# Embedding outputs copied by ScalarE, an earlier bank wait for two products, and norm splits moved, in a two-layer hybrid encoder step on one core

## The chip, the cores and the metric

The kernel runs on one core of one Trainium2 chip. The metric is the device time of one execution in microseconds, as the median of several runs. TensorE multiplies, VectorE (DVE) and ScalarE (ACT) work element by element and read TensorE's results out of PSUM, GpSimd (POOL) works on SBUF only, and SyncE (SP) issues nearly all DMAs. Each engine runs its own instructions in the order of the program and waits on semaphores that the others raise.

## The reference

544 tokens (512 of a prompt and 32 of a sample) of width 1024 pass through two layers. A layer is

```
x = x + concat(A, B, C, D) @ w_out          # four mixers on rmsnorm(x) @ w_in
x = x + square(relu(rmsnorm(x) @ mlp_w1)) @ mlp_w2                   # 1024 -> 4096 -> 1024
x = x + (pl @ ple_w_proj) * sigmoid(rmsnorm(x) @ ple_w_gate)         # pl: 256 wide, one per layer
```

and a final rmsnorm gives y. All is float32. The change touches the end of the second line and the third one, the embedding block.

## The kernel before, in words

x lies in SBUF with features on partitions, as 8 tiles of 128x544 (tile m holds features 128m to 128m+127). A weight matrix is cut in units of 128 output features: a unit is 128x1024 float32, loaded by SP (`load_unit`, L675) into one of four raw places. Each float32 value is split in a high part (fp32r, made by ScalarE: `high`, L893, which waits for the product two units before to have left the place) and a remainder (made by POOL from raw and high: `rest`, L775). Activations are split likewise: `norm_high` (ACT, L958) scales a tile of x by the norm's gain, `norm_split` (DVE, L1237) makes the remainder; `square_x` (ACT, L964) and `add_square` (POOL, L801) gather the sum of squares, which TensorE sums over partitions (`sum_x`) and ScalarE turns into 1/rms (`inv_rms`, L970: a logarithm read from PSUM and an exponential); the product is multiplied by it afterwards. The two tiles of squares alternate, so square m waits until POOL has added square m-2.

A product (`product`, L1724) takes for each of 8 input tiles three matmul pairs (high by high, high by remainder, remainder by high; two halves of 272 tokens): 48 matmuls. Its output takes two of the four banks of psum_p, so outputs alternate between two slots, and output o waits for the evacuation of output o-2 (`evacuated`, L640, a count on the semaphore `freed`).

The MLP runs in 4 groups of 1024 hidden features. A group has 8 such products into psum_p and then 4 pairs (p = 0 to 3) of output tiles, each from seven half-size products (K_A11, K_S1, K_S2, K_S4, K_S3, K_A12, K_A22, in this order, 12 matmuls each: `pair_product`, L1762) into the four banks of the other PSUM tensor, psum_t, each waiting for the evacuation of the one four before. VectorE evacuates and adds them into x tiles 2p and 2p+1 (L1576 to L1598; A11 is copied by ScalarE, L915), and between them makes the weight sums for the next pair (`pair_sum`, L1520). A12 completes tile 2p, A22 tile 2p+1. In the last group VectorE also makes the norm splits for the embedding block, two in each of the pairs 1 to 3 (behind S2 and S4), and splits 6 and 7 at the end.

Then the embedding block, outputs from O_PLE on. Outputs 0 to 3 are products of the embedding with `ple_w_proj` (12 matmuls each, unit U_PLE), 4 to 7 gate products 0 to 3 (48 matmuls each, units U_PLE+1 to U_PLE+4), 8 to 11 again embedding products (U_PLE+5), 12 to 15 gate products 4 to 7. VectorE copies embedding outputs to `ple_out` (L1695, five tiles in turn), multiplies a gate output by 1/rms (L1702), ScalarE takes the sigmoid (L1208), VectorE multiplies by the embedding and adds to x (`add_gated`, L1680). ScalarE then squares the new x tile and, in layer 0, scales it for layer 1, and VectorE makes layer 1's split.

All orders are written out by hand in one function for each engine. POOL's order in the last group is: remainders due, then in pair p the sums of squares 2p-2 and 2p-1, with U_PLE's remainder ahead of sum 4, and U_PLE+1's behind sum 5. In layer 0 SP loads, behind U_PLE+2, the next layer's parameters (waiting for the last split) and 1088 KB of constants (L757), and then U_PLE+3.

## Time and profile before

| | us |
|---|---|
| runs (3), median | 1614.86 (1613.15 to 1617.97) |
| profiled execution, time | 1612.89 |
| profiled execution, span | 1611.1 |
| TensorE busy | 1525.2 (95%) |
| VectorE busy | 1050.8 (65%) |
| POOL busy | 832.0 (52%) |
| ScalarE busy | 670.0 (42%) |

The mean granted TensorE clock was 0.988 of full speed. The embedding block of layer 0 lies at about 736 to 805 us of the span, that of layer 1 at 1528 to 1594 us. In timelines a row gives start, duration, engine, line, what is written and read, how many instructions are merged, and in brackets the idle time before it with what ended it.

### The profile page before, as it was taken

The page shows a single profiled execution, that of the slowest core. Times are in us where ns is not written, and L with a number is a line of the kernel's source. Part 1 is how long each engine was busy: PE and PEld are TensorE (multiplying, and loading weights), DVE is VectorE, ACT ScalarE, POOL GpSimd, SP SyncE. Part 2 cuts the span into 40 slices and gives each one's busy share as a digit, 9 for nine tenths or more (in the row PEclk, how much of TensorE's full clock was granted, in tenths as well). Part 3 has the DMA queues.
Part 4 walks back from the last instruction along what each step waited for, and adds up shares of the span by engine and source line. Part 5 has one row for each costly group of instructions (what it writes and reads, how often), then busy time and mean ns, then how long its engine had stood idle before and what let it go on. Part 6 is the DMA issues. An engine that isn't in the chain of part 4 may idle for free.

```text
span 1611.1 us, 33871 instructions
## 1 busy us (share of the span) xinstructions
PE 1525.2 (95%) x14198; PEld 1439.6 (89%) x14198; DVE 1050.8 (65%) x1754; ACT 670.0 (42%) x1186; POOL 832.0 (52%) x467
## 2 busy tenths in 40 slices
PE   6999999899999999998999999998999999999896
PEld 6889787799999999988998897878999999999895
DVE  6865557656848567596677645664487584756954
ACT  6521433335544343453455223342454443434522
POOL 3344111165766849486543431112759486684943
PEclk9999999999999999999999999999999999999998
DMA  5211001152241414213322110113333224141221
GB/s 197 79 41 42 27 28 40 46 133 92 79 132 53 132 53 118 80 53 100 104 67 67 41 39 17 41 40 73 113 97 96 89 79 132 53 133 51 66 80 69
DMA packets 43960, 123.81 MB, mean 77 GB/s; under 512 B 10976, under 2 KB 13792, under 8 KB 43552
## 3 DMA queue, kind: packets, MB, share of 16 engines
q1 hardware_dynamic: 43664, 119.86, 24.1%
q8 instruction: 113, 1.85, 0.5%
q10 hardware_dynamic: 144, 1.78, 0.3%
q14 instruction: 39, 0.32, 0.1%
HBM read 117.86 MB, written 3.76 MB: 75 GB/s over the span
## 4 chain that ended last, share of the span: by engine, by line
PE 73%; DVE 18%; issue 3%; ACT 3%; POOL 1%; DMA 0%; SPq 0%; POOLq 0%; DVEq 0%; ACTq 0%
PE psum_p L1736 37%; PE psum_t L1777 16%; PE psum_p L1791 5%; PE psum_t L1827 5%; DVE conv_out L1277 2%; DVE hidden L1241 2%; PE psum_p L1970 1%; PE psum_p L1950 1%; PE psum_p L1756 1%; PE psum_t L1943 1%; PE psum_t L1938 1%; POOL w_rest L779 1%; DVE probs L1491 1%; DVE x L1588 1%; DVE mla_q L1308 1%
## 5 line engine op out<-in xcount | busy, mean ns | idle before, releaser
L1736 PE MATMUL psum_p<-hidden,w_high 128*128 128x272 f32 x3776 | 637.6, 291 | 10.9 <-POOL w_rest L779 8.6
L1736 PEld LDWEIGHTS psum_p<-hidden,w_high 128*128 128x128 f32 x3776 | 537.0, 189 | 15.6 <-POOL w_rest L779 10.3
L779 POOL TENSOR_TENSOR w_rest<-raw,w_high 128x1024 fp32r<-128x1024 f32 x114 | 280.5, 2464 | 464.9 <-ACT w_high L899 464.9
L1736 PE MATMUL psum_p<-hidden,w_rest 128*128 128x272 f32 x1888 | 391.2, 289 | 0.0
L1736 PEld LDWEIGHTS psum_p<-hidden,w_rest 128*128 128x128 f32 x1888 | 296.9, 189 | 0.0
L791 POOL TENSOR_TENSOR w_rest<-w_sums,w_high 128x512 fp32r<-128x512 f32 x128 | 207.7, 1648 | 93.3 <-DVE w_sums L1533 55.3
L899 ACT ACTIVATE w_high<-raw 128x1024 fp32r<-128x1024 f32 x114 | 120.1, 1055 | 192.4 <-PE psum_p L1736 115.4
L1777 PE MATMUL psum_t<-hidden_split_a,w_high 128*128 128x272 f32 x896 | 178.5, 290 | 12.8 <-issue 7.7
L1777 PE MATMUL psum_t<-hidden_split_b,w_high 128*128 128x272 f32 x896 | 177.1, 288 | 0.4 <-DVE hidden_split_b L1549 0.4
L1777 PEld LDWEIGHTS psum_t<-hidden_split_a,w_high 128*128 128x128 f32 x896 | 140.0, 188 | 17.3 <-issue 17.1
L1777 PEld LDWEIGHTS psum_t<-hidden_split_b,w_high 128*128 128x128 f32 x896 | 140.3, 188 | 0.8 <-DVE hidden_split_b L1549 0.8
L1777 PE MATMUL psum_t<-hidden_split_b,w_rest 128*128 128x272 f32 x448 | 128.9, 288 | 0.0
L1777 PE MATMUL psum_t<-hidden_split_a,w_rest 128*128 128x272 f32 x448 | 128.8, 288 | 0.0
L913 ACT ACTIVATE w_high<-w_sums 128x512 fp32r<-128x512 f32 x128 | 79.6, 628 | 118.0 <-DVE w_sums L1531 62.4
L1557 DVE SCALAR_TENSOR_TENSOR rope_in<-psum_p,rms 128x544 f32<-128x544 f32 x64 | 46.2, 722 | 114.8 <-PE psum_p L1736 102.7
L779 POOL TENSOR_TENSOR w_rest<-raw_more,w_high 128x1024 fp32r<-128x1024 f32 x32 | 80.4, 2521 | 54.1 <-ACT w_high L899 54.1
L1241 DVE SCALAR_TENSOR_TENSOR hidden<-x,parameters,hidden 128x544 fp32r<-128x544 f32 x48 | 78.6, 1642 | 32.7 <-ACT hidden L962 32.0
L938 ACT ACTIVATE hidden_parts<-rope_in 128x544 f32<-128x544 f32 x64 | 42.2, 659 | 127.7 <-DVE rope_in L1557 127.7
L1791 PE MATMUL psum_p<-hidden,w_high 128*128 128x272 f32 x512 | 91.2, 300 | 0.1
L791 POOL TENSOR_TENSOR w_rest<-raw,w_high 128x512 fp32r<-128x512 f32 x48 | 75.0, 1570 | 29.0 <-ACT w_high L913 29.0
L1777 PEld LDWEIGHTS psum_t<-hidden_split_b,w_rest 128*128 128x128 f32 x448 | 84.3, 188 | 0.0
L1777 PEld LDWEIGHTS psum_t<-hidden_split_a,w_rest 128*128 128x128 f32 x448 | 84.3, 188 | 0.0
(289 smaller groups left out, 2578.0 us busy)
## 6 DMA issues: line engine op xcount, KB each, us to landing
raw<-w_units SPq DMA_DIRECT2D x146, 512.0 KB, 3.6
raw_more<-w_units SPq DMA_DIRECT2D x64, 512.0 KB, 3.6
x<-x_t SPq DMA_DIRECT2D x8, 272.0 KB, 6.3
y_t<-y SPq DMA_DIRECT2D x8, 272.0 KB, 2.1
constants<-consts ACTq DMA_DIRECT2D x1, 1737.5 KB, 8.1
ple_in<-p_t SPq DMA_DIRECT2D x2, 544.0 KB, 11.0
constants<-consts SPq DMA_DIRECT2D x1, 1088.0 KB, 5.3
w_kv<-w_kv SPq DMA_DIRECT2D x2, 256.0 KB, 5.2
```

The source lines that it names most:

```text
L779: mark(pool.tensor_tensor(wlo_at(l, s, 2), raw_at(l, u), whi_at(l, s, 2).bitcast(F32), ALU.subtract), lo_done)
L791: mark(pool.tensor_tensor(wlo_at(l, s, 1), src, whi_at(l, s, 1).bitcast(F32), ALU.subtract), lo_done)
L899: mark(act.activation(whi_at(l, place_of(u), 2), raw_at(l, u), ACT.Copy), hi_done)
L913: mark(act.activation(whi_at(l, s, 1), src, ACT.Copy), hi_done)
L938: link(act, act.activation(dst, two(xr[:]), ACT.Square), h_sq, l)
L1241: mark(dve.scalar_tensor_tensor(ha[l][:, m, 1, :], x[:, m, :], g, f(ha[l][:, m, 0, :]), ALU.mult, ALU.subtract), normed)
L1277: step(dve.scalar_tensor_tensor(dst, src[:, j:j + cols], w, dst, ALU.mult, ALU.add), l)
L1557: link(dve, dve.scalar_tensor_tensor(two(xr[:]), psum_of(l, o), 0.0, two(rms[:]), ALU.max, ALU.mult), freed, l)
L1736: ins = pe.matmul(pp[:, 2 * b + h, 0:HALF], w(l, s, 2)[:, cols(k)], rhs[:, k, part, h * HALF:(h + 1) * HALF], start=(n == 0 and z == 0), s ...
L1777: ins = pe.matmul(bank, w(l, s, 1)[:, j * P:(j + 1) * P], hs(l, j)[:, half, part, :], start=(j == 0 and z == 0), stop=(j == PAIRS - 1 and ...
L1791: ins = pe.matmul(pp[:, h, 0:HALF], w(l, s, 2)[:, k * P:(k + 1) * P], ha[l][:, k, half, h * HALF:(h + 1) * HALF], start=(k == 0 and z == 0 ...
L1827: ins = pe.matmul(dst[r, j * C:(j + 1) * C], lhsT(r), rhs(r), start=True, stop=True)
```

## The change

- `copy_ple` is new: ScalarE copies embedding output m from PSUM to `ple_out` and signals `ple_copied`. Copies 0 to 3 stand around the scaling and squaring of x tiles 6 and 7, copies 4 to 7 in the loop over gates behind the sigmoid of gate 3 (4 and 5) and behind the square and scaling of tile 3 (6 and 7). VectorE's copies go; `add_gated` of tile 3 moves to its own turn.
- `evacuated` counts the embedding outputs on `ple_copied`, and the first two embedding products wait for the last hidden product of the last group, the last reader of psum_p, instead of the outputs two before them.
- The splits of tiles 0 to 5 in the last group stand at (pair 1, S4), (2, S2), (2, S4), (3, S2), (3, S4), (3, S3) instead of two in each pair; POOL adds square 5 behind U_PLE+1's remainder instead of ahead of it.

```diff
@@ -473,7 +473,7 @@
         lo_done = signal("lo_done", O_PLE + 2 + KT, 4)
         sums = signal("sums", 4 * PAIRS * GROUPS)
         proj = signal("proj", OUTPUTS, 2)
-        freed = signal("freed", OUTPUTS - PAIRS * GROUPS, 2)
+        freed = signal("freed", OUTPUTS - PAIRS * GROUPS - KT, 2)
         x_high = signal("x_high", 3 * KT)
         normed = signal("normed", 3 * KT, 1)
 
@@ -554,7 +554,7 @@
         ple_hi = signal("ple_hi", 1)
         copied = signal("copied", PAIRS * GROUPS)
         ple_sp = signal("ple_sp", 1)
-        ple_o = signal("ple_o", 2 * KT)
+        ple_copied = signal("ple_copied", KT)
         gate_in = signal("gate_in", KT)
         gated = signal("gated", KT)
         yd = signal("yd", 0)
@@ -644,6 +644,9 @@
             for g in range(GROUPS):
                 for p in range(PAIRS):
                     before += pair_out(g, p, K_A11) <= o
+            if O_PLE <= o < O_PLE + 4 or O_PLE + 8 <= o < O_PLE + 12:
+                return ple_copied.at(l, o - O_PLE + 1 - (4 if o >= O_PLE + 8 else 0))
+            before += (4 if o >= O_PLE + 4 else 0) + (4 if o >= O_PLE + 12 else 0)
             return freed.at(l, o + 1 - before)
 
         def square_no(phase, m):
@@ -864,8 +867,10 @@
                         rest_of(l, due(g, 2 * KT + 7 * p, ahead))
                         if g == GROUPS - 1 and p:
                             add_square(l, 2, 2 * p - 2)
-                            add_square(l, 2, 2 * p - 1)
+                            if p < PAIRS - 1:
+                                add_square(l, 2, 2 * p - 1)
                         rest_of(l, due(g, 2 * KT + 7 * p + ahead, 7 - ahead))
+                add_square(l, 2, KT - 3)
                 add_square(l, 2, KT - 2)
                 add_square(l, 2, KT - 1)
                 u = U_PLE + SPLIT
@@ -919,6 +924,12 @@
                     q = PAIRS * g + p - 1
                     act.wait_ge(*evacuated(l, pair_out(q // PAIRS, q % PAIRS, K_S4)))
                 mark(act.activation(pq[:, 0, :], pair_bank(g, p, K_A11), ACT.Copy), copied)
+
+            def copy_ple(l, m):
+
+                o = O_PLE + m + (4 if m >= 4 else 0)
+                act.wait_ge(*proj.at(l, o + 1))
+                mark(act.activation(two(pout[:, m % 5, :]), out_of(l, o), ACT.Copy), ple_copied)
 
             def high_of(l, work):
 
@@ -1189,9 +1200,14 @@
                                 for m in (2 * p - 2, 2 * p - 1):
                                     norm_high(l, 2, m)
                                     square_x(l, 2, m)
-                for m in (KT - 2, KT - 1):
-                    norm_high(l, 2, m)
-                    square_x(l, 2, m)
+                copy_ple(l, 0)
+                copy_ple(l, 1)
+                norm_high(l, 2, KT - 2)
+                square_x(l, 2, KT - 2)
+                copy_ple(l, 2)
+                norm_high(l, 2, KT - 1)
+                square_x(l, 2, KT - 1)
+                copy_ple(l, 3)
                 for m in range(KT):
                     if m % 4 == 0:
                         high(l, U_PLE + SPLIT + 5 * (m // 4))
@@ -1206,12 +1222,18 @@
                         high(l + 1, u - UNITS)
                     act.wait_ge(*gate_in.at(l, m + 1))
                     mark(act.activation([xr, sqt][m % 2][:], [xr, sqt][m % 2][:], ACT.Sigmoid), gated)
+                    if m == 3:
+                        copy_ple(l, 4)
+                        copy_ple(l, 5)
                     if m < KT - 1:
                         square_x(l, 3, m)
                         if l + 1 < DEPTH:
                             if m == 0:
                                 act.wait_ge(*gains_in.at(l + 1, 16))
                             norm_high(l + 1, 0, m)
+                    if m == 3:
+                        copy_ple(l, 6)
+                        copy_ple(l, 7)
 
             act.preload_act_table_set(nat)
             square_x(DEPTH, 0, KT - 1)
@@ -1549,6 +1571,8 @@
                 mark(dve.tensor_tensor(hs(l, j)[:, 1, a:b, :], hq[:, a:b, :], f(hs(l, j)[:, 0, a:b, :]), ALU.subtract),
                      hidden)
 
+            norms = {(1, K_S4): 0, (2, K_S2): 1, (2, K_S4): 2, (3, K_S2): 3, (3, K_S4): 4, (3, K_S3): 5}
+
             def mlp_group(l, g):
                 for i in range(KT):
                     o = mlp_out(g, i)
@@ -1594,8 +1618,8 @@
                             dst = {K_S4: x[:, m, HALF:TOK], K_A12: x[:, m, 0:HALF], K_A22: x[:, m + 1, 0:HALF]}[k]
                             link(dve, dve.tensor_tensor(dst, bank, dst, ALU.add), freed, l)
                         sums_of(l, due(g, 2 * KT + 7 * p + k, 1))
-                        if g == GROUPS - 1 and p and k in (K_S2, K_S4):
-                            norm_split(l, 2, m - 2 + (k == K_S4))
+                        if g == GROUPS - 1 and (p, k) in norms:
+                            norm_split(l, 2, norms[p, k])
                 if g == GROUPS - 1:
                     norm_split(l, 2, KT - 2)
                     norm_split(l, 2, KT - 1)
@@ -1684,25 +1708,18 @@
                             dve.wait_ge(*gains_in.at(l + 1, 16))
                         norm_split(l + 1, 0, m - 1)
                     dve.wait_ge(*gated.at(l, m + 1))
+                    dve.wait_ge(*ple_copied.at(l, m + 1))
                     step(dve.tensor_tensor(gate, gate, pout[:, m % 5, :], ALU.mult), l)
                     link(dve, dve.tensor_tensor(x[:, m, :], x[:, m, :], gate, ALU.add), x_new, l)
 
                 for m in range(KT):
-                    if m % 4 == 0:
-                        for j in range(4):
-                            o = O_PLE + 2 * m + j
-                            dve.wait_ge(*proj.at(l, o + 1))
-                            link(dve, dve.tensor_copy(two(pout[:, (m + j) % 5, :]), psum_of(l, o)), freed, l)
-                        if m:
-                            add_gated(m - 1)
-                        if m == 0:
-                            dve.wait_ge(*rms_ready.at(l, 3))
+                    if m == 0:
+                        dve.wait_ge(*rms_ready.at(l, 3))
                     o = O_PLE + 4 * (m // 4 + 1) + m
                     dve.wait_ge(*proj.at(l, o + 1))
                     link(dve, dve.tensor_tensor(two([xr, sqt][m % 2][:]), psum_of(l, o), two(rms[:]), ALU.mult), freed, l)
                     mark(dve.memset(t1[:, 0:1], 0.0), gate_in)
-                    if m % 4 < 3 or m == KT - 1:
-                        add_gated(m)
+                    add_gated(m)
 
             dve.wait_ge(rms_ready.sem, DEPTH * rms_ready.per + 1)
             for m in range(KT):
@@ -1725,7 +1742,7 @@
 
                 b, s = slot(l, o), place_of(u)
                 pe.wait_ge(*lo_done.at(l, weight_no(u) + 1))
-                pe.wait_ge(*evacuated(l, o - 2))
+                pe.wait_ge(*evacuated(l, mlp_out(GROUPS - 1, KT - 1) if o in (O_PLE, O_PLE + 1) else o - 2))
                 for n, k in enumerate(order):
                     if between is not None and n == len(order) // 2:
                         between()
```

## Rows read from the trace of the kernel before

**Rows 1.** The page, its parts 1 and 4, whole span: busy time by engine; last chain.
```profile
PE 1525.2 (95%) x14198; PEld 1439.6 (89%) x14198; DVE 1050.8 (65%) x1754; ACT 670.0 (42%) x1186; POOL 832.0 (52%) x467
...
PE 73%; DVE 18%; issue 3%; ACT 3%; POOL 1%; DMA 0%; SPq 0%; POOLq 0%; DVEq 0%; ACTq 0%
```

**Rows 2.** Timeline of TensorE, layer 1: start us, us, what, count, idle before and releaser.
```profile
1513.97 0.49 PE L1777 MATMUL psum_t<-hidden_split_a,w_high 128*128 128x272 f32 x2 [1.52 <-DVE x L1595]
...
1525.02 0.29 PE L1777 MATMUL psum_t<-hidden_split_b,w_rest 128*128 128x272 f32 x1
1528.30 0.74 PE L1736 MATMUL psum_p<-ple_split,w_high 128*128 128x272 f32 x4 [2.99 <-DVE x L1595]
...
1531.44 1.11 PE L1736 MATMUL psum_p<-ple_split,w_high 128*128 128x272 f32 x4
...
1534.38 0.74 PE L1736 MATMUL psum_p<-ple_split,w_high 128*128 128x272 f32 x4 [1.37 <-DVE ple_out L1695]
...
1537.44 0.67 PE L1736 MATMUL psum_p<-hidden,w_high 128*128 128x272 f32 x4
...
1543.21 0.41 PE L1736 MATMUL psum_p<-hidden,w_rest 128*128 128x272 f32 x2
...
1575.48 0.77 PE L1736 MATMUL psum_p<-hidden,w_high 128*128 128x272 f32 x4 [0.85 <-POOL w_rest L779]
```

**Rows 3.** Windows, layer 1: stretch, us, busy (count) by engine, clock, DMA share, GB/s.
```profile
1530.00:1532.00 2.00, 2.00 (x11) 2.00 (x10) 2.00 (x2) 0.67 (x2) 2.00 (x2) 0.50 0.00 0
```

**Rows 4.** Timeline of VectorE, layer 1.
```profile
1500.09 1.34 DVE L1241 SCALAR_TENSOR_TENSOR hidden<-x,parameters,hidden 128x544 fp32r<-128x544 f32 x1
...
1521.26 1.77 DVE L1241 SCALAR_TENSOR_TENSOR hidden<-x,parameters,hidden 128x544 fp32r<-128x544 f32 x1
...
1523.42 2.48 DVE L1241 SCALAR_TENSOR_TENSOR hidden<-x,parameters,hidden 128x544 fp32r<-128x544 f32 x1
...
1527.71 0.92 DVE L1595 TENSOR_TENSOR x<-psum_t,x 128x272 f32<-128x272 f32 x2
1529.04 4.55 DVE L1241 SCALAR_TENSOR_TENSOR hidden<-x,parameters,hidden 128x544 fp32r<-128x544 f32 x2 [0.41 <-ACT hidden L962]
```

**Rows 5.** Timeline of POOL, layer 1.
```profile
1522.42 2.90 POOL L779 TENSOR_TENSOR w_rest<-raw,w_high 128x1024 fp32r<-128x1024 f32 x1
...
1531.18 3.61 POOL L811 TENSOR_TENSOR x_squares_summed<-x_squares_summed,x_squared 128x544 f32<-128x544 f32 x2
1538.84 2.39 POOL L779 TENSOR_TENSOR w_rest<-raw,w_high 128x1024 fp32r<-128x1024 f32 x1 [4.05 <-ACT w_high L899]
```

**Rows 6.** Timeline of ScalarE, layer 1.
```profile
1523.11 1.05 ACT L899 ACTIVATE w_high<-raw 128x1024 fp32r<-128x1024 f32 x1
...
1537.70 1.06 ACT L899 ACTIVATE w_high<-raw 128x1024 fp32r<-128x1024 f32 x1 [7.03 <-PE psum_p L1736]
1544.58 0.71 ACT L973 ACTIVATE rms<-psum_t,constants 128x544 f32<-128x544 f32 x1 [5.82 <-PE psum_t L1721]
...
1563.68 0.64 ACT L1208 ACTIVATE squares<-squares 128x544 f32<-128x544 f32 x1
```

**Rows 7.** Instructions on ple_out, both layers: duration ns min/median/max, first and last start.
```profile
L1695 DVE COPY ple_out<-psum_p x16: 711/725/726, 741.6 to 1568.7; 128x544 f32<-128x544 f32 x16
...
L1687 DVE TENSOR_TENSOR squares<-squares,ple_out x8: 721/2474/2753, 761.7 to 1595.5; 128x544 f32<-128x544 f32 x8
```

**Rows 8.** Timeline of VectorE, layer 0.
```profile
771.28 0.72 DVE L1702 TENSOR_TENSOR squares<-psum_p,rms 128x544 f32<-128x544 f32 x1
```

**Rows 9.** Part 6 of the page, and SP's queue, layer 0: the constants' transfer.
```profile
constants<-consts SPq DMA_DIRECT2D x1, 1088.0 KB, 5.3
...
742.04 0.43 SPq L757 DMA_DIRECT2D constants<-consts  x1
```

**Rows 10.** Timeline of TensorE, layer 0.
```profile
784.70 0.77 PE L1736 MATMUL psum_p<-hidden,w_high 128*128 128x272 f32 x4 [1.81 <-POOL w_rest L779]
...
785.60 1.11 PE L1736 MATMUL psum_p<-hidden,w_high 128*128 128x272 f32 x4
```

## The prediction

> **What bounds the kernel now.** I read the page's busy shares first: TensorE is busy 95% of the span, and the chain that ended last is 73% TensorE and 18% VectorE [rows 1]. So time is to be had only where TensorE stands still, and I looked for that around the edited code: the last MLP group and the embedding block, which run once in each of the two layers, at 690 to 805 us and at 1480 to 1594 us. The layers agree in what follows to about 0.1 us after a shift of 792 us; I work in layer 1's times.
>
> TensorE's timeline there [rows 2] shows four larger stops. A pair product is 12 matmuls in about 1.5 us (the last ends at 1525.31). At 1513.97 it has waited 1.52 us for a VectorE evacuation. The first embedding product starts only at 1528.30, 2.99 us after it, released by an evacuation into x, though it writes a bank of the other PSUM tensor. After the stop the second product runs at half clock: in 1530 to 1532 the granted clock is 0.50, the lower level, 1.2 GHz [rows 3]. Then TensorE stands 1.37 us until VectorE has copied the first product out; products 3 and 4 take 1534.38 to 1537.4, and gate product 0 takes 1537.44 to 1543.45, so 6.02 us for 48 matmuls. From 1525.31 to 1537.44 are 12.13 us, in which TensorE has 48 matmuls, 6.02 us of work. The fourth stop, 0.85 us at 1575.48 (about 1.1 by the starts of the matmuls), waits for POOL's weight remainder.
>
> Why VectorE is late is in its rows [rows 4]: in this stretch hardly one has idle time before it, evacuations, weight sums and norm splits in a row. At the end, 1529.04 to 1533.6, it runs splits 6 and 7 (4.55 us for both) before it takes the first embedding copy.
>
> **The change, part by part.**
>
> *New wait for the first two products.* They wait for the bank's last reader, the evacuation of the last hidden product, some 50 us back. What is late next is the weight remainder of U_PLE: POOL writes it at 1522.42 to 1525.32, and POOL's rows here, as those before them, have no idle time in front, down to 1534.79 [rows 5]. So TensorE can start at about 1525.4 instead of 1528.30: 2.9 us gained. Nothing else is queued behind that wait but the following products.
>
> *Splits spread.* Splits 0 to 5 sat at two each in pairs 1, 2, 3; now one, two, three, the last behind the S3 addition. Pair 1 loses one split, 1.34 us by its row [rows 4]. VectorE has a backlog there, so every evacuation up to pair 2's last comes up to 1.34 us earlier and the pair products end at about 1524.0. That buys nothing as long as POOL delivers U_PLE at 1525.3; it is cover for POOL's being quicker where VectorE is idle (gain 0 to 0.3 us, I take 0). The added split falls between the S3 addition and the A12 evacuation: 1.34 to 2.48 us by the neighbours; I take 1.77, the split at 1521.26 with POOL beside it [rows 4]. Net of the 1.34 us before it, x tiles 6 and 7 come at 1528.6 and 1529.1 instead of 1528.15 and 1528.63.
>
> *Copies on ScalarE.* The trace has no ScalarE copy of 128x544 from PSUM with this form; nearest is the logarithm out of PSUM, 0.71 us [rows 6]; VectorE's copies take 0.711 to 0.726 [rows 7]. I take 0.71 (bounds 0.64, the sigmoid of the same shape [rows 6], and 0.75). ScalarE is in order: U_PLE+1's high part is done at 1524.15. Product 1 runs 1525.4 to 1526.9, copy 0 to 1527.8; product 2 to 1528.4, copy 1 to 1529.35; product 3 starts at 1528.4 and product 4 at 1529.9, both without a stop. Scaled tile 6 (0.7) and its square (0.6) then run to 1530.65, copy 2 to 1531.35. Gate product 0 needs that bank: 1531.5, where TensorE is free at 1531.45. Splits 6 and 7 end at about 1532.3 and 1534.5 and are needed 4.5 and 5.3 us into gate 0, at 1536.0 and 1536.8: covered. POOL: square sum 4 to 1527.1, U_PLE+1's remainder to 1529.7 (now ahead of sum 5), sums 5, 6, 7 to 1534.9, U_PLE+2's remainder (2.39) to 1537.3; wanted at 1538.2 after the sum of squares. Covered by 0.9 us. So gate 0 starts 5.95 us earlier than 1537.44.
>
> *Second four embedding products.* Gate 3 ends near 1562.5 (1543.45, the sum of squares 0.7, three gates and a slower restart of 0.2). Copies 4 and 5 follow the sigmoid of tile 3 (ends 1564.32) and keep up. Copies 6 and 7 sit behind the square of x tile 3, which waits for VectorE's gate multiply, 2.5 us beside POOL [rows 7], and its addition: 1567.6, square 1568.3, copy 6 at 1569.0. Gate 4 then starts 0.65 us late. In exchange VectorE no longer holds x tile 3 back behind its four copies, to about 1571, so U_PLE+7 is converted in time and the stop at 1575.48 (1.1 us) goes. Net gain 0.45. Layer 1 in all: 5.95 + 0.45 = 6.4 us; its tail after the last gate is unchanged.
>
> *Layer 0 differs* in this block, since VectorE also makes the next layer's splits and multiplies take up to 2.75 us beside POOL [rows 7]: it reaches gate 3's output at 771.28, late by 0.8 us against 770.5, gate 3's end [rows 8]. And the constants' transfer, issued at 742.04 behind the last split, stands in front of U_PLE+3's load [rows 9]; the last split now ends about 1.0 us later (742.6), so, with 5.3 us for the constants and an estimated 0.5 for the rest of the load behind them, the load lands near 748.9, while ScalarE, after the rms (1544.58 and 1.4 us, less the two shifts), wants it at 748.05. That shifts the multiply chain by 0.85 us. With it I get stops of 0.3 (U_PLE+5's remainder), 0.7, 1.25 (copy 4 after a late sigmoid) and 1.2 us (copy 6 behind square and scaled tile 3), together 3.45, where today are 0.35 at product 2 and at gate 5 a stop of 1.81 us followed by 3.6 us at low clock, some 1.7 lost [rows 10]: 3.9. Gain 0.45 minus 0.1 for gate 2, plus 5.95 before it: 6.2 us.
>
> Sum: 6.4 + 6.2 = 12.6; I take off 0.3 for semaphore latencies that I rounded away: 12.3. The profiled execution took 1612.89 us (span 1611.1), so 1600.6; the runs' median, 1614.86, lies 2 us above it, and 12.3 below the median is 1602.5.
>
> On the splits beside POOL: the rows show 1.34 and 2.48 us for one shape. The Trainium skill (SBUF — State Buffer, "Who interferes with whom") says that a VectorE instruction with two SBUF inputs and a GpSimd instruction that reads SBUF lock each other out for a whole instruction. By it the added split could wait for one whole weight remainder and take 2.5 us instead of 1.77; copy 2 and gate 0 would be 0.7 us later in each layer, 1.4 in all, and the time 1603.9.
>
> **Rivals.**
>
> *A, the clock falls all the same.* TensorE would still stand about 1.4 us before the first product. For: 1.81 us before 784.70 was enough, the clock fell 0.6 us after it [rows 10]. Against: 1.52 us at 1513.97 was not [rows 2]. Price: at low clock six matmuls take 1.36 us instead of 0.75 (a group of four 1.11 against 0.67) [rows 2]; the stretches lasted 3.6 us, 1.6 to 1.8 us lost each. Once per layer, and once for layer 0's stops at the second four: 5.0 us, time 1607.5.
>
> *B, a queue is behind.* POOL has no gap, and U_PLE+2's remainder has 0.9 us of slack only. If it came as now, 1541.23, gate 1 would start 1541.3 instead of 1538.2: 3.1 us lost per layer, gain 12.3 - 6.2 = 6.1, time 1608.8. Against: that time is set today by the 7.03 us ScalarE waits for the product [rows 6], which goes.
>
> *C, no change.* The copies do not keep up: if ScalarE reached copies 0 and 1 only behind tiles 6 and 7, product 3 would again wait until about 1532.5, and the second four would lose the rest. The program order puts them first, so this is that the change doesn't do what it says. Time 1614.
>
> *D, slower.* The stops of layer 0 at the second four are close together (0.7, 1.25, 1.2 us between products of 1.5 us). If they hold the clock at 1.2 GHz not for 3.6 us but through gates 4 to 7, each gate takes 10.9 us instead of 6.02: 19.5 us more, time 1622. It decides from 12.3 / 0.81 = 15 us of TensorE work, two and a half gates, done at the low level. Against: both falls in this stretch ended after 3.6 us, once work went on.
>
> **How the numbers follow.** Forecast 64% (own range 1599 to 1605.5), A 19%, B 9%, C 4%, D 4%. Range for 8 in 10: below to 1598.5 (POOL quicker by 0.3 per layer, copies at 0.64, the median's own scatter of 2 us), above to 1608, which takes in A. 0.3% of the time is about 4.8 us, what a measurement here can tell from no change: faster is the forecast, A, and B: 0.92; same 0.04; slower 0.04.
>
> **What would show it.** After: the first embedding product within 0.3 us of U_PLE's remainder, no 2.99 us stop and no clock of 0.50 there; four copies on ScalarE at 0.7 us; gate 0 about 6 us after the first product; the 1.52 us stop at pair 3 near 0.2; a stop of about 0.7 us ahead of gate 4 in layer 1 and of three about 1 us in layer 0; no stop ahead of gate 5. Wrong would be: first product not before 1528 (another release), copies over 1 us, gate 1 waiting for POOL, or a low clock for long.

## The result and the profile after

The changed kernel took 1604.33 us (median of 6 runs, 1600.98 to 1606.62) where the kernel before took 1613.8 (6 runs, 1611.09 to 1617.97): a ratio of 0.9936, interval 0.9922 to 0.995. Once more, on another occasion (e11 below), it was 1603.55 us and 0.9938 [0.9926, 0.9951]. So it is faster by some 10 us, where 12.3 were forecast. The profiled execution took 1600.98 us (span 1599.2), 11.9 less than the profiled one of before, and is the quickest of its six. Of the five executions of e5 below one took 3071.51 us: the median given there counts it, the ratio leaves it out, and the median of the other four is 1600.08 us.

First the page of the changed kernel, its parts 1 and 4, as [rows 1] of before: TensorE has 8.2 us less busy time with the same 14198 matmuls; most of it is time at the lower clock that is gone (6.8 us of clock less, by the sums under e11); VectorE has 16 instructions less, ScalarE 16 more.

```profile
PE 1517.0 (95%) x14198; PEld 1433.4 (90%) x14198; DVE 1041.9 (65%) x1738; ACT 678.2 (42%) x1202; POOL 832.2 (52%) x467
...
PE 72%; DVE 18%; ACT 5%; issue 3%; DMA 1%; POOL 1%; SPq 0%; POOLq 0%; DVEq 0%; ACTq 0%
```

TensorE's timeline in layer 1, to be laid beside [rows 2]. Its columns are start us, duration us, engine, line, what, count, and in brackets the idle time before and its releaser.

```profile
1506.53 0.49 PE L1794 MATMUL psum_t<-hidden_split_a,w_high 128*128 128x272 f32 x2 [1.60 <-DVE x L1619]
...
1517.59 0.29 PE L1794 MATMUL psum_t<-hidden_split_b,w_rest 128*128 128x272 f32 x1
1519.65 0.75 PE L1753 MATMUL psum_p<-ple_split,w_high 128*128 128x272 f32 x4 [1.78 <-issue]
1520.23 0.41 PE L1753 MATMUL psum_p<-ple_split,w_rest 128*128 128x272 f32 x2
...
1525.71 0.67 PE L1753 MATMUL psum_p<-hidden,w_high 128*128 128x272 f32 x4
...
1557.56 0.74 PE L1753 MATMUL psum_p<-hidden,w_high 128*128 128x272 f32 x4 [0.68 <-ACT ple_out L932]
```

The reader should see four things. The stop in front of the first embedding product is 1.78 us and no longer 2.99. The first four embedding products, 48 matmuls, run in 6.06 us without a stop (1519.65 to 1525.71). The stop before pair 3 (1506.53) has stayed. The granted clock, which was 0.50 in this place before [rows 3], is 1.00 (a window: stretch, its length, busy time and count by engine, clock, DMA share, GB/s):

```profile
1520.00:1522.00 2.00, 2.00 (x19) 2.00 (x18) 1.97 (x3) 0.57 (x1) 2.00 (x2) 1.00 0.54 162
```

What releases the first product reads "issue", which names nothing. GpSimd's timeline gives it: the remainder of weight unit U_PLE ends at 1519.55, 0.1 us before the product.

```profile
1513.09 3.66 POOL L814 TENSOR_TENSOR x_squares_summed<-x_squares_summed,x_squared 128x544 f32<-128x544 f32 x2
1516.71 2.84 POOL L782 TENSOR_TENSOR w_rest<-raw,w_high 128x1024 fp32r<-128x1024 f32 x1
1519.50 1.85 POOL L814 TENSOR_TENSOR x_squares_summed<-x_squares_summed,x_squared 128x544 f32<-128x544 f32 x1
1521.31 2.90 POOL L782 TENSOR_TENSOR w_rest<-raw,w_high 128x1024 fp32r<-128x1024 f32 x1
```

ScalarE's timeline shows the copies, each behind its product, and in the second four the square of tile 3 in front of the last two; the row under them is from the view by tile, with durations in ns (min/median/max) of all sixteen:

```profile
1521.43 0.63 ACT L932 ACTIVATE ple_out<-psum_p 128x544 f32<-128x544 f32 x1 [2.98 <-PE psum_p L1753]
1522.92 0.63 ACT L932 ACTIVATE ple_out<-psum_p 128x544 f32<-128x544 f32 x1 [0.87 <-PE psum_p L1753]
...
1556.24 0.66 ACT L979 ACTIVATE x_squared<-x 128x544 f32<-128x544 f32 x1 [1.69 <-DVE x L1713]
1556.81 1.12 ACT L932 ACTIVATE ple_out<-psum_p 128x544 f32<-128x544 f32 x2
...
L932 ACT ACTIVATE ple_out<-psum_p x16: 602/616/627, 736.7 to 1557.3; 128x544 f32<-128x544 f32 x16
```

Layer 0's second four products have stops of the kind that was forecast, at TensorE; there is none ahead of gate 5, where [rows 10] had 1.81 us:

```profile
768.44 0.74 PE L1753 MATMUL psum_p<-ple_split,w_high 128*128 128x272 f32 x4 [0.43 <-DVE squares L1720]
...
771.01 0.74 PE L1753 MATMUL psum_p<-ple_split,w_high 128*128 128x272 f32 x4 [0.85 <-ACT ple_out L932]
...
775.80 0.74 PE L1753 MATMUL psum_p<-hidden,w_high 128*128 128x272 f32 x4 [1.56 <-ACT ple_out L932]
```

Absolute times drift between executions, so I count from the first pair product of the last MLP group (1477.56 in layer 1 before, 1471.77 after). From there the places of one kernel agree within 0.1 us in both layers and in each profile, but for e1's gate 0. For every kernel of this study (us after that product; worked out from TensorE's timelines; layer 0 / layer 1 where they differ):

| kernel | pairs end | first product | gate 0 |
|---|---|---|---|
| before | 47.75 | 50.7 | 59.85 |
| changed | 46.1 | 47.85 | 53.9 |
| e1, wait alone | 47.8 | 47.85 | 62.35 / 61.3 |
| e2, copies alone | 47.75 | 50.7 | 59.5 |
| e3, change with the old splits | 47.75 | 47.85 | 53.9 |
| e4, splits alone | 46.1 | 50.6 | 58.55 |
| e6, e8, e12 | 46.1 | 46.1 | 52.5 |
| e9, old splits on e8 | 47.75 | 47.6 | 53.75 |
| e10, split 1 later on e8 | 46.0 | 46.1 | 52.5 |

(e5, e7 and e11 stand as the changed kernel.) VectorE's multiply of the last gate came 119.0 and 116.4 us after the start before, 113.2 and 110.2 after: 5.84 us gained in layer 0 and 6.13 in layer 1, together 12.0. That the two profiles differ by as much, 11.9, is luck: outside these stages there are differences of about 2 us both ways (under e11).

### The profile page after: what moved, and what is told of

Same layout as the page of the kernel before. It is cut to its first block, busy times and chain, and to the rows that moved or that the text cites. A ratio compares the mean times of both kernels' runs of the same rounds, so it can differ in the third digit from the quotient of the medians.

```text
span 1599.2 us, 33873 instructions
## 1 busy us (share of the span) xinstructions
PE 1517.0 (95%) x14198; PEld 1433.4 (90%) x14198; DVE 1041.9 (65%) x1738; ACT 678.2 (42%) x1202; POOL 832.2 (52%) x467
## 3 DMA queue, kind: packets, MB, share of 16 engines
q10 hardware_dynamic: 144, 1.78, 0.3%
## 4 chain that ended last, share of the span: by engine, by line
PE 72%; DVE 18%; ACT 5%; issue 3%; DMA 1%; POOL 1%; SPq 0%; POOLq 0%; DVEq 0%; ACTq 0%
PE psum_p L1753 35%; PE psum_t L1794 17%; PE psum_p L1808 5%; PE psum_t L1844 5%; DVE conv_out L1299 2%; PE psum_p L1773 1%; PE psum_p L1987 1%; PE psum_p L1967 1%; PE psum_t L1960 1%; PE psum_t L1955 1%; ACT w_high L904 1%; DVE probs L1513 1%; DVE squares L1712 1%; DVE w_sums L1559 1%; DVE mla_q L1330 1%
## 5 line engine op out<-in xcount | busy, mean ns | idle before, releaser
L1263 DVE SCALAR_TENSOR_TENSOR hidden<-x,parameters,hidden 128x544 fp32r<-128x544 f32 x48 | 75.0, 1565 | 32.8 <-ACT hidden L973 32.2
L794 POOL TENSOR_TENSOR w_rest<-raw,w_high 128x512 fp32r<-128x512 f32 x48 | 75.1, 1570 | 29.0 <-ACT w_high L918 29.0
```

Of the source, the lines that this page charges most:

```text
L794: mark(pool.tensor_tensor(wlo_at(l, s, 1), src, whi_at(l, s, 1).bitcast(F32), ALU.subtract), lo_done)
L1263: mark(dve.scalar_tensor_tensor(ha[l][:, m, 1, :], x[:, m, :], g, f(ha[l][:, m, 0, :]), ALU.mult, ALU.subtract), normed)
```

## The experiments

The first four take the change apart, each on the same chip beside the kernel before (1613.18 us, median of 25 runs). The next four alter one thing in the changed kernel or all three together (before: 1613.05, 9 runs), the last four follow up (before: 1613.66, 11 runs).

**e1: the new wait alone**, in the kernel before.

```diff
-                pe.wait_ge(*evacuated(l, o - 2))
+                pe.wait_ge(*evacuated(l, mlp_out(GROUPS - 1, KT - 1) if o in (O_PLE, O_PLE + 1) else o - 2))
```

> The kernel before with one edit: the first two embedding products wait for the last hidden product's evacuation. Copies stay on VectorE, splits stay two in each pair. My theory (the parts need each other): the first two products move up to U_PLE's remainder at about 1525.4, but product 3 waits as before for VectorE's first copy, which stands behind splits 6 and 7 that end at 1533.6; TensorE stands about 6 us in one piece there instead of 2.99 + 1.37, the clock falls to 0.50 behind it and gate 0 starts where it did or up to 1.8 us later. Time 0 to 4 us above before, ratio 1.000 to 1.002. Rival (each part gives its own share): the 2.9 us at the first product are gained in each layer, time 5.8 us below before, ratio 0.996.

Measured: 1617.92 us, ratio 1.0029 [1.0015, 1.0042]: slower. TensorE's timeline in layer 1 and a window of it:

```profile
1526.93 0.74 PE L1736 MATMUL psum_p<-ple_split,w_high 128*128 128x272 f32 x4
...
1535.88 1.25 PE L1736 MATMUL psum_p<-ple_split,w_high 128*128 128x272 f32 x4 [5.72 <-DVE ple_out L1695]
```
```profile
1537.00:1539.00 2.00, 2.00 (x11) 2.00 (x11) 0.00 (x0) 0.00 (x0) 0.00 (x0) 0.50 0.00 0
```

The first two products start at once when the pairs end. But VectorE's copies still stand behind the evacuations and splits 6 and 7, so TensorE stands 5.72 us in one piece in front of the third, and the work behind it runs at the clock of 0.50, 1.2 GHz. The windows show that clock for 6.8 us, from 1532.3 to 1539.1, where the kernel before has it for 3.4 us in this place; gate 0 comes 1.4 to 2.5 us later than before, which is more than I had expected. The wait alone moves a stop and makes it cost more.

**e2: the copies on ScalarE alone.** The cut shows two places of the edit to the kernel before.

```diff
+                copy_ple(l, 0)
+                copy_ple(l, 1)
...
-                            link(dve, dve.tensor_copy(two(pout[:, (m + j) % 5, :]), psum_of(l, o)), freed, l)
```

> The changed kernel with the other two parts undone: ScalarE's copies only; the first products wait for the outputs two before, splits two in each pair. My theory: the first product still starts near 1528.3 (layer 1, times of the kernel before), 3 us stop and low clock as before (some 1.3 us), then products 3 and 4 follow without the stop of 1.37 and the wait behind the splits: gate 0 near 1535.7 instead of 1537.44, 1.7 us gained; at the second four 0.45 in layer 1 and up to 2 in layer 0. Together 5 to 6 us below before, ratio 0.9965. Rival (the copies carry the whole gain and the early wait is only shifted waiting): as the changed kernel, ratio 0.9936.

Measured: 1611.47 us, 0.9991 [0.9978, 1.0004]. I had expected 0.9965, a miss. TensorE and a window:

```profile
1525.69 1.25 PE L1751 MATMUL psum_p<-ple_split,w_high 128*128 128x272 f32 x4 [2.94 <-DVE x L1617]
1526.73 0.66 PE L1751 MATMUL psum_p<-ple_split,w_rest 128*128 128x272 f32 x2
1527.18 1.11 PE L1751 MATMUL psum_p<-ple_split,w_high 128*128 128x272 f32 x4
```
```profile
1529.00:1531.00 2.00, 2.00 (x10) 2.00 (x10) 0.00 (x0) 0.41 (x1) 0.00 (x0) 0.50 0.63 166
```

The stop of 2.94 us is there, the stop for the copy (1.37 us in [rows 2]) is gone. But the clock is at 0.50 from the first product on and each four matmuls take 1.11 us for 0.66, so the four products need 8.8 us and not 6.05. The windows give a granted clock of 0.50 for 6.8 us (1524.9 to 1531.7), 6.0 of them with work, at a cost of 2.75 us. In the kernel before it is 0.50 for 3.4 us only (1529.5 to 1532.9), a cost of 1.7; it begins 1.2 us behind the start of the first product, and it is over when the second stop comes:

```profile
1533.00:1535.00 2.00, 0.63 (x6) 0.66 (x6) 1.95 (x3) 0.00 (x0) 1.64 (x2) 1.00 0.48 176
```

So 1.0 of the 1.37 us that the copies win goes into a longer stretch at the lower clock, and gate 0 gains 0.35 us. Layer 0 shows the same 6.8 and 3.4 us. The stop in front is as long in both kernels (2.94 and 2.99 us); why the stretch is twice as long in e2 is not shown.

**e3: the changed kernel with the splits at their old places.** GpSimd's sum 5 goes back ahead of the unit's remainder too, which the cut leaves out.

```diff
-            norms = {(1, K_S4): 0, (2, K_S2): 1, (2, K_S4): 2, (3, K_S2): 3, (3, K_S4): 4, (3, K_S3): 5}
+            norms = {(1, K_S2): 0, (1, K_S4): 1, (2, K_S2): 2, (2, K_S4): 3, (3, K_S2): 4, (3, K_S4): 5}
```

> The changed kernel with the splits back at two in each of pairs 1 to 3 and square 5 added ahead of U_PLE+1's remainder. My theory: POOL's remainder of U_PLE, not the end of the pair products, lets the first embedding product start, so the spread of the splits is worth nothing: pair products end 1.2 us later, the first product starts at the same time relative to the group's start, within 0.3 us of the changed kernel per layer; the stop before it shrinks from 1.78 to about 0.4 us. Ratio to before 0.9925 to 0.9945. If long stops now and then drop the clock in the changed kernel (its six runs lie in two groups, 1601 to 1603 and 1606 to 1607), this one has fewer of the slow ones. Rival (the spread matters): 1.2 us per layer lost, ratio 0.995 or above.

Measured: 1601.88 us, 0.9929 [0.991, 0.9948], not to be told from the change. The pairs end 1.65 us later, the first product starts at the same 47.85 us:

```profile
1519.24 0.29 PE L1792 MATMUL psum_t<-hidden_split_b,w_rest 128*128 128x272 f32 x1
1519.62 0.74 PE L1751 MATMUL psum_p<-ple_split,w_high 128*128 128x272 f32 x4
```

None of its four runs (1600.94 to 1602.13) is near 1606, as I had expected if the stop mattered; e6 below speaks against it. So the wait and the copies are the gain, and only as a pair: the ratios of e1 and e2 multiply to 1.0020.

**e4: the splits alone.** The same line of norms (and GpSimd's sum 5 behind the unit's remainder) in the kernel before.

> The kernel before with the splits' new places and POOL's new order alone. My theory: the pair products end 1.2 us earlier, but the first embedding product still waits for the A12 evacuation, which comes 0.0 to 0.5 us later than before because a split stands in front of it: time 0 to 1.5 us above before, ratio 1.000 to 1.001. Rival (the spread matters by itself): 1.2 us per layer gained, ratio 0.9985.

Measured: 1611.45 us, 0.9986 [0.9972, 1.0], which leaves the rival standing. Splits 6 and 7 on VectorE took 3.37 us for two, not 4.55 [rows 4], so the first copy came sooner; gate 0 gains 1.3 us in each layer. I had given this part nothing.

```profile
1530.98 3.37 DVE L1243 SCALAR_TENSOR_TENSOR hidden<-x,parameters,hidden 128x544 fp32r<-128x544 f32 x2 [0.41 <-ACT hidden L964]
```

**e5: the second four copies in one row**, in the changed kernel. The two lines go away in their old place, which the cut leaves out.

```diff
                     if m == 3:
                         copy_ple(l, 4)
                         copy_ple(l, 5)
+                        copy_ple(l, 6)
+                        copy_ple(l, 7)
```

> The changed kernel with one edit: ScalarE copies the second four embedding products one behind the other, 6 and 7 directly behind 4 and 5, ahead of the square and the scale of tile 3. My theory says that the stop in front of gate 4 (0.68 us in layer 1, 0.85 and 1.56 us in layer 0 of the changed kernel) is the two operations of 0.6 to 1.1 us between copies 5 and 6, so the stops go and each layer gains 0.7 to 1.5 us: 2 us of 1604, a ratio to the kernel before of 0.9925 where the change alone had 0.9936. Rival 1: what is late next is the square of tile 3 and through it the gate, VectorE then stops for ScalarE, and nothing is gained (0.9936). Rival 2: the stops are short enough to cost their own length only and the rest is other jitter, 0.9930.

Measured: 1601.39 us, 0.9924 [0.9908, 0.9939]. ScalarE's copies now stand one behind the other, and gate 4 has no stop in either layer, 0.85 us sooner in layer 1 and 1.74 in layer 0, as expected. The other stop for a copy in layer 0, 0.84 us before the third of the four products, stays. The comparison with 0.9936 alone would not tell it; the timeline does.

```profile
1551.94 0.63 ACT L932 ACTIVATE ple_out<-psum_p 128x544 f32<-128x544 f32 x1 [0.82 <-PE psum_p L1752]
1553.43 0.62 ACT L932 ACTIVATE ple_out<-psum_p 128x544 f32<-128x544 f32 x1 [0.87 <-PE psum_p L1752]
1554.92 0.63 ACT L932 ACTIVATE ple_out<-psum_p 128x544 f32<-128x544 f32 x1 [0.87 <-PE psum_p L1752]
```

**e6: the unit's remainder ahead of sum 3** on GpSimd, and ScalarE's square 5 behind its second copy. The cut shows GpSimd's part.

```diff
+                            if p == PAIRS - 1:
+                                add_square(l, 2, 2 * p - 3)
...
-                            if p < PAIRS - 1:
+                            if p < PAIRS - 2:
```

> The changed kernel with one edit in two places: GpSimd takes the embedding unit's remainder (2.90 us) ahead of the sum of square 3 (1.85 us), and ScalarE's square 5 goes behind its second copy. My theory says that the first embedding product's stop of 1.78 us at the end of the pairs is the place of that remainder in GpSimd's queue: it ends 1.85 us sooner, the stop goes in both layers, and gate 0 comes sooner by what the sums of squares allow. Time: 1.8 us by two layers less if the whole of it arrives, a ratio of 0.991 to 0.992; and the lower clock, which I take for the cause of the slower half of the changed kernel's runs (1606 against 1601 us, mean clock 0.989 against 0.992), should not be seen, so that all of its runs are near 1598. Rival 1: VectorE's splits decide the start of gate 0 (they end at the same time as before), the stop moves behind the eighth product, and the ratio stays at 0.9936. Rival 2: the slower half has nothing to do with this stop, and is seen here too.

Measured: 1601.31 us, 0.9922 [0.9907, 0.9937]. The stop of 1.78 us is gone: on TensorE the first product now follows the last pair product, and has no idle time in its row.

```profile
1514.05 0.29 PE L1798 MATMUL psum_t<-hidden_split_b,w_rest 128*128 128x272 f32 x1
1514.34 0.75 PE L1757 MATMUL psum_p<-ple_split,w_high 128*128 128x272 f32 x4
```

Of the 1.75 us, gate 0 keeps 1.4 (52.5 against 53.9), and 0.6 more is lost by the end of gate 3, where TensorE now stops 0.22 us for the next remainder and restarts slower. The slower half of its runs is there still (1600.6 to 1602.6 at a mean clock near 0.989, the quick one 1596.4 at 0.993). So rival 2 of this expectation holds: my idea that this stop lets the clock fall in half of the runs is wrong. At the last gate 0.6 us is left in layer 0 and 1.1 in layer 1, not 1.8 in each.

**e7: the next layer's loads one unit later.**

```diff
-                    if u == U_PLE + 2 and l + 1 < DEPTH:
+                    if u == U_PLE + 3 and l + 1 < DEPTH:
```

> The changed kernel with one edit: SyncE issues the next layer's parameters and constants one unit later, behind the transfer of the raw weights that ScalarE waited for in layer 0 (0.69 us). My theory prices this at 0 to 0.7 us, since it comes once in the kernel and ScalarE's work there is not what TensorE waits for last: ratio 0.9934, not to be told from the change (0.9936). The rival, that this transfer's lateness is what puts the stops of 0.4 to 1.6 us into layer 0 behind its second four products, expects them gone and 2.5 us less: 0.992.

Measured: 1601.45 us, 0.9929 [0.9916, 0.9942]. In the timelines of ScalarE, layer 0, the wait for the raw weights is in the changed kernel's row and not in e7's:

```profile
750.18 1.06 ACT L904 ACTIVATE w_high<-raw 128x1024 fp32r<-128x1024 f32 x1 [0.69 <-DMA raw<-w_units]
```
```profile
749.40 1.05 ACT L904 ACTIVATE w_high<-raw 128x1024 fp32r<-128x1024 f32 x1
```

Of the stops in layer 0's second four, the two in front of the first and the second product (0.24 and 0.43 us) go, those for a copy stay at 0.83 and 1.56 us. Gate 4 comes 0.8 us sooner, about what my theory priced.

**e8: e5, e6 and e7 together.**

> The changed kernel with the three edits together: four copies in one row, the embedding unit's remainder ahead of sum 3, the next layer's loads one unit later. If the stops are separate places, their gains add: 2 us of the copies, 3.6 us of the remainder, up to 0.7 us of the loads, so 1598 us and a ratio of 0.990. If the sums of squares or VectorE take the place of each stop that goes, it stays at 0.993.

Measured: 1594.77 us (1592.47 to 1598.76), 0.989 [0.9872, 0.9908]. The gains add: counted at the last gate, e5, e6 and e7 gain 1.8, 0.6 and 0.8 us over the change in layer 0 and 0.9, 1.1 and 0.0 in layer 1, 5.2 in sum, and e8 gains 3.9 and 1.8, so 5.7. **e12, the same kernel again** beside the change:

> The kernel with three further edits once more, on the same chip as the change: 0.989 to the kernel before and 9 to 10 us below the change if the first comparison was right, which had 4 runs alone; between 0.990 and 0.991 if its two quick runs were luck.

Measured: 1595.52 us, 0.9895 [0.9877, 0.9913]; it lies 8.0 us below the changed kernel on the same chip, where the last gates give 5.7; the rest is not explained by these stages. It beats both kernels.

**e9: e8 with the splits at their old places** (the edit of e3).

> The kernel with the three further edits, with the norm splits of the last group at their old places (pairs' products 1_S2, 1_S4, 2_S2, 2_S4, 3_S2, 3_S4) again. In the changed kernel the new places were worth nothing, since GpSimd's remainder set the first embedding product whenever the pairs ended. My theory says that with the remainder out of the way the pairs' end sets it, so the old places now cost what they delay it by, 1.2 us in each layer: 2.4 us more than the kernel with three edits, a ratio of 0.9905 against its 0.989. The rival, that VectorE has the same work before gate 0 whatever its order, expects gate 0 at the same distance from the group's start and the same time, 0.989.

Measured: 1597.91 us, 0.9908 [0.9894, 0.9923], 2.4 us slower than e12 on the same chip, where the two intervals overlap. The timelines decide: pairs end at 47.75, gate 0 at 53.75 against 52.5, and the last gate comes 1.2 us later in layer 0 and 0.7 in layer 1. So the new places of the splits are worth 1.2 us at gate 0, and 1.9 us in the two layers together, from the moment the stop behind them goes, and nothing before.

**e10: e8 with split 1 behind S4 and split 2 behind S3.**

```diff
-            norms = {(1, K_S4): 0, (2, K_S2): 1, (2, K_S4): 2, (3, K_S2): 3, (3, K_S4): 4, (3, K_S3): 5}
+            norms = {(1, K_S4): 0, (2, K_S4): 1, (2, K_S3): 2, (3, K_S2): 3, (3, K_S4): 4, (3, K_S3): 5}
```

> The kernel with the three further edits, with VectorE's split 1 moved from behind pair 2's product S2 to behind its S4, and split 2 to behind S3. TensorE stops 1.58 us in front of pair 3 for an addition that stands behind split 1 (1.69 us) in VectorE's order. If the order is what counts, the stop goes and each layer gains up to 1.6 us: a ratio of 0.987 against 0.989. If VectorE's work paces the pairs, smaller stops in pair 3 take it over and the pairs end no more than 0.3 us sooner: 0.989. The second is what the changed kernel did with its splits, and I give it two chances in three.

Measured: 1598.76 us (1592.86 to 1602.24), 0.9908 [0.9893, 0.9924], not to be told from e12 by the intervals; the last gates stand where e12's do, within 0.1 us. The stop in front of pair 3 went, and one of 1.69 us came in front of that pair's third product; the pairs end 0.1 us sooner:

```profile
1507.91 0.49 PE L1797 MATMUL psum_t<-hidden_split_a,w_high 128*128 128x272 f32 x2
...
1512.99 0.49 PE L1797 MATMUL psum_t<-hidden_split_a,w_high 128*128 128x272 f32 x2 [1.69 <-DVE x L1622]
```

The first row is the start of pair 3, 33.14 us after the group's first pair product (34.73 in e8), with no idle time. So the order of these two splits decides where TensorE stands still, and VectorE's work as a whole when the pairs end: the second case of the expectation, but for the one stop of the old length where I had expected smaller ones.

**e11: the changed kernel again.**

> The changed kernel once more, beside the kernel with three further edits on the same chip. Expected: 0.9936 again, runs from 1600 to 1607 us. The clock's falls outside the embedding stage lie at other places in every profile so far (25, 245, 260, 310, 340, 815, 1100 us), each worth some 1.7 us; if they are what spreads the runs of one kernel over 5 us, this profile shows other places than the first one did, and its time stands to the first profile's as their number does. If something in the embedding stage spreads the runs, both profiles differ there.

Measured: 1603.55 us, 0.9938 [0.9926, 0.9951]. In both its profiles the clock is 1.00 all through the embedding stage. The expectation's second half is a miss. This profile has the first one's falls (at 310, 815 and 1100 us) and one more at 260; by the sums below it loses 3.4 us more to the clock, and yet it took 0.4 us less (1600.57 against 1600.98 us). One place where the lost time is made up lies in layer 0. At 323 us this execution is 2.2 us behind the first one (325.46 against 323.29 us for the same product). Then both wait for a weight remainder in front of one product, the first execution for 3.30 us and this one for 0.77, since ScalarE gets the raw weights of that unit at nearly the same time in both (335.38 and 334.98 us):

```profile
338.91 0.77 PE L1753 MATMUL psum_p<-hidden,w_high 128*128 128x272 f32 x4 [3.30 <-POOL w_rest L782]
```
```profile
338.55 0.77 PE L1753 MATMUL psum_p<-hidden,w_high 128*128 128x272 f32 x4 [0.77 <-POOL w_rest L782]
```

So time lost to the clock can vanish in a later wait for weights, and the clock is not all that counts. Most of what spreads the runs is outside the embedding stage, best seen in the two profiles of e8 and e12, one kernel, 9.2 us apart (1593.03 and 1602.23). Windows of e8:

```profile
28.00:30.00 2.00, 2.00 (x10) 2.00 (x10) 1.96 (x4) 1.98 (x3) 2.00 (x1) 0.50 0.53 217
340.00:345.00 5.00, 5.00 (x42) 5.00 (x42) 2.75 (x2) 1.33 (x3) 3.38 (x3) 1.00 0.36 116
1100.00:1105.00 5.00, 4.69 (x38) 4.47 (x36) 2.15 (x2) 2.46 (x4) 2.09 (x1) 1.00 0.00 0
```

and of e12:

```profile
28.00:30.00 2.00, 2.00 (x18) 2.00 (x18) 1.96 (x4) 1.98 (x3) 2.00 (x1) 1.00 0.58 234
340.00:345.00 5.00, 5.00 (x28) 5.00 (x29) 3.70 (x3) 2.30 (x3) 5.00 (x3) 0.66 0.33 107
1100.00:1105.00 5.00, 5.00 (x30) 4.53 (x30) 0.45 (x2) 0.29 (x2) 0.00 (x0) 0.50 0.45 77
```

Summed over windows of 5 us up to the last gates, (1 - clock) times 5 us gives 5.1 us lost in e8's profile and 15.4 in e12's, a difference of 10.3 where the times differ by 9.2. (It counts idle time in a window too, so it is an upper estimate.) The same sum, in the embedding stages of both layers (715 to 800, 1500 to 1570 us) and elsewhere: before 5.1 and 6.8; e1 6.9 and 6.8; e2 6.8 and 6.7; e4 5.2 and 10.2; the change 0 and 5.1, again (e11) 0 and 8.5; e3 0 and 6.8; e5 to e10 0 and 3.4 to 13.6. In all 14 profiles the clock falls between 305 and 320 us and between 1090 and 1110 us; the other places differ from one execution to the next. Each is worth 1.7 us or more by this sum, and only those of the embedding stage belong to the change.

## Why the prediction was right, and where it was not

**New wait, first product at the remainder's end: right.** 2.9 us were forecast; the first product moved from 50.7 to 47.85 us after the group's start. GpSimd's remainder ends at 47.8 us in both kernels.

**Splits spread, earlier pairs worth nothing: right for the change.** e3 shows the same first product and gate 0 without it. The pairs end 1.65 us sooner, not 1.2 to 1.34. The step "the 1.52 us stop at pair 3 near 0.2" is wrong: it is 1.60 us, and e10, which takes it away in front of pair 3, gets it back inside that pair; what vanished in the change are the smaller stops in front of and within pair 2, some 1.7 us in all. With the old kernel's copies the part is worth more than I saw (e4), and with the remainder out of the way too (e9).

**Copies on ScalarE, gate 0 5.95 us earlier: right.** 5.95 by the table. The copies take 0.60 to 0.63 us, not 0.71. e1 and e2 show that this gain is neither part's own: one gives GpSimd's time as the start, the other takes the copies off VectorE, and alone each leaves a long stop with a low clock behind it.

**Second four, layer 1: a stop of 0.65 before gate 4 and none before gate 5: right**, 0.68 and none. **Layer 0: right in kind.** Forecast 0.3, 0.7, 1.25 and 1.2 us; from the starts of the matmuls 0.24, 0.6, 1.0 and 1.74. e7 shows which of them hang on the late load (0.69 us at ScalarE, 0.85 forecast): the first two. e5 shows that the last is the square and the scaled tile in front of copy 6.

**The sum, 12.3 us: near in the edited stages, 2 to 3 us too much for the medians.** The stages give 5.84 and 6.13, so 12.0. (The prediction's own terms for layer 0, 0.45 - 0.1 + 5.95, make 6.3 and not 6.2.) The term that came out small is the second four: in layer 1 the stops and the stop that goes leave 0.19 us where 0.45 was forecast, in layer 0 they leave 0.14 for 0.45, and 0.27 is lost ahead of them where 0.1 was. The gain is at the first four alone.

The medians differ by 9.5 and 10.1. What they lack lies outside the edited stages, which the prediction took as equal in both kernels. The clock there is the likeliest cause and not a proven one: it costs 3.4 to 15.4 us in one execution and another, and among the six executions of the change the time goes with the mean clock (0.993 took 1600.98 us; 0.991 took 1601.29 and 1602.74; 0.990 took 1605.92; 0.989 took 1606.18 and 1606.62). A single profile of before says little of it. Whether the change also makes these falls likelier is open; 14 profiles do not tell. The two profiled executions agree with the stages' 12.0 by luck: the changed kernel's loses 1.7 us less to the clock outside them, and waits 2.1 us longer for the weights at 338 us (3.30 against 1.18). Luck helps the forecast time as well: 1602.5 was counted from a median of three runs, 1614.86, that lies 1.1 to 1.8 us above the later ones.

**Rivals.** A, the clock falls all the same: no, in neither profile of the changed kernel nor in those of e3 and e5 to e10. B, a queue behind: GpSimd's U_PLE+2 remainder began at 1529.09 and gate 1 had no stop. C and D did not come about. A's price may have been too low: the stretch at the lower clock, which the prediction took as 3.6 us, is 3.4 by the windows in the kernel before, but 6.8 in e1 and e2. The stop of 1.78 us is as long as the one of 1.81 us in [rows 10] behind which the clock fell, and in e1 a stop of 1.81 us at the place of [rows 10] left the clock at 1.00; what tells them apart is not shown here.

**The split beside GpSimd.** Before, a split that starts at 1523.42 ends at 1525.90, 0.58 us after the remainder beside it, which ends at 1525.32 [rows 4, 5]. In the changed kernel VectorE's rows read:

```profile
1515.91 1.42 DVE L1263 SCALAR_TENSOR_TENSOR hidden<-x,parameters,hidden 128x544 fp32r<-128x544 f32 x1
1517.25 0.43 DVE L1614 TENSOR_TENSOR pair_parts<-psum_t,pair_parts 128x272 f32<-128x272 f32 x1
1517.72 2.42 DVE L1615 TENSOR_TENSOR x<-x,pair_parts 128x544 f32<-128x544 f32 x1
1520.17 1.77 DVE L1263 SCALAR_TENSOR_TENSOR hidden<-x,parameters,hidden 128x544 fp32r<-128x544 f32 x1
```

They end at 1517.33, 1520.14 and 1521.94 us. GpSimd's instruction under way when each began ends at 1516.75, 1519.55 and 1521.35: each is 0.58 or 0.59 us after it. So the added split took 1.77 us, the value of the sum, since it met a sum of squares and not a remainder. The remainder met the addition before it, which took 2.42 us for 1.39 before, while the split before that took 1.42 for 2.48: the long wait changed hands, and the 1.77 us came out right partly by luck. The Trainium skill (SBUF — State Buffer, "Who interferes with whom") says that two such instructions lock each other out for a whole instruction; these rows agree. The prediction's 2.5 us was the right rule with the wrong neighbour: in these rows the price is what is left of GpSimd's instruction.

## What to carry to other kernels

A wait that is moved forward pays only if what stands behind it is freed by then: alone the new wait cost 0.3%, with the copies moved it is the larger part of 0.6%. Before valuing an edit at nothing, say what covers it, and try it again when that cover goes (e3 and e9: 0 and 1.2 us at gate 0 for the same line). Where the clock falls at changing places, count each stage from a mark inside it and read its gain there; a comparison of medians alone could not have told e5, e6 and e7 from the change, and their timelines could.

## What the runs showed of the hardware

- The same stop does not always bring the clock down: e8 and e12 both stand 2.34 us before 27.8 us and go on with the same matmuls; the granted clock behind it is 0.50 in the one, 1.00 in the other (the windows at 28 us above). TensorE's row behind that stop in e8, and then in e12:

```profile
27.82 1.25 PE L1756 MATMUL psum_p<-hidden,w_high 128*128 128x272 f32 x4 [2.34 <-DVE misc L1283]
```
```profile
27.74 0.73 PE L1756 MATMUL psum_p<-hidden,w_high 128*128 128x272 f32 x4 [2.34 <-DVE misc L1283]
```

- The same holds of a stop of 1.81 us in front of gate 5 in layer 0: the clock behind it is 0.50 for 3.4 us in the kernel before [rows 10], and 1.00 in e1, whose row is

```profile
789.78 0.77 PE L1736 MATMUL psum_p<-hidden,w_high 128*128 128x272 f32 x4 [1.81 <-POOL w_rest L779]
```

- The stretch at the lower clock behind the first embedding product's stop is not of one length: 3.4 us in the kernel before, 6.8 in e2 behind an equally long stop. It costs what work falls into it: in e2 the four products took 8.8 us, in the changed kernel 6.05.
- A copy of 128x544 from PSUM takes 0.62 us on ScalarE, against 0.71 to 0.73 on VectorE [rows 7].
- A VectorE instruction with two SBUF inputs that runs beside one of GpSimd ended 0.58 or 0.59 us after it in the four places above.
